# Norm factors spread from eight columns, the causal mask moved into VectorE's scan, and row 0 of each attention item scored half an item further ahead

## The reference, cut to what matters

```python
def rmsnorm(x, g):
    y = x * lax.rsqrt(jnp.mean(x * x, axis=-1, keepdims=True) + EPS)
    return y * g
# stick-breaking, for a block of queries at positions t
mask = key_pos[None, :] < t[:, None]
z = jnp.einsum("bhqd,bhkd->bhqk", qb, kf) * scale
log_keep = jnp.where(mask, jax.nn.log_sigmoid(-z), 0.0)
later = lax.cumsum(log_keep, axis=3, reverse=True) - log_keep
log_a = jax.nn.log_sigmoid(z) + later
a = jnp.where(mask, jnp.exp(log_a), 0.0)
out = jnp.einsum("bhqk,bhkd->bhqd", a, vf)
```

## Time and profile before

| | us |
|---|---|
| device time, median of 3 runs | 2651.57 (2646.75 to 2653.51) |
| span of the profiled execution, first to last instruction | 2646.9 |
| TensorE busy in that span | 2562.6 (97%) |
| VectorE, ScalarE, GpSimd busy | 1784.0, 1204.7, 719.9 |
| mean granted TensorE clock | 0.989 |

### The profile page before, as it was taken

The page is one execution under the profiler, slowest core; times in us unless marked ns, Lnnn a source line. Parts: engine busy times, 40 slices in busy tenths (PEclk is TensorE's granted clock), DMA queues, the critical chain, the costliest instruction groups (busy, mean ns, idle before and its releaser), DMA issues.

```text
span 2646.9 us, 34791 instructions
## 1 busy us (share of the span) xinstructions
PE 2562.6 (97%) x12320; PEld 2130.7 (80%) x12320; DVE 1784.0 (67%) x2247; ACT 1204.7 (46%) x2027; POOL 719.9 (27%) x523
## 2 busy tenths in 40 slices
PE   8899999999999999999999999998899999999999
PEld 8688887888888887887878888886788888887887
DVE  6566666167756577775677777777648665758667
ACT  6463333144434443335666666665424443444332
POOL 2502220102323222233033333333120322222322
PEclk9899999999999999999999999999999999999999
DMA  6412225213433456534111111112321342437634
GB/s 208 152 40 72 78 90 191 80 63 116 146 116 119 151 177 246 217 147 159 49 37 33 33 32 32 32 32 107 125 101 53 139 161 77 152 133 273 236 145 157
DMA packets 85923, 311.39 MB, mean 118 GB/s; under 512 B 10417, under 2 KB 10417, under 8 KB 73137
## 3 DMA queue, kind: packets, MB, share of 16 engines
q1 hardware_dynamic: 74304, 261.17, 28.0%
q0 software_dynamic: 11216, 42.47, 4.5%
q10 hardware_dynamic: 288, 6.29, 0.6%
HBM read 220.24 MB, written 89.65 MB: 117 GB/s over the span
## 4 chain that ended last, share of the span: by engine, by line
PE 79%; DVE 7%; issue 7%; ACT 4%; POOL 1%; DMA 1%; SPq 0%; ACTq 0%; DVEq 0%; POOLq 0%
PE ps L2334 25%; PE ps L2336 24%; PE ps L2335 24%; PE ps L2646 1%; POOL sig L968 1%; DVE aT_lo L1955 1%; PE ps L2662 1%; DVE tile_lo L2203 1%; DVE w_lo L1584 1%; DVE keep L1913 1%; ACT keep L1313 1%; PE ps L2663 1%; PE ps L2595 1%; ACT sq L1325 1%; PE ps L2596 1%
## 5 line engine op out<-in xcount | busy, mean ns | idle before, releaser
L2334 PE MATMUL ps<-tile_hi,g_hi 128*128 128x512 f32 x1680 | 661.3, 394 | 7.7 <-DVE tile_lo L2203 5.2
L2336 PE MATMUL ps<-tile_hi,g_lo 128*128 128x512 f32 x1680 | 658.3, 392 | 0.0
L2335 PE MATMUL ps<-tile_lo,g_hi 128*128 128x512 f32 x1680 | 654.7, 390 | 0.0
L2334 PE MATMUL ps<-xg_hi,w_hi 128*128 128x512 f32 x1024 | 412.6, 403 | 4.5 <-DVE xg_lo L1783 3.3
L2336 PE MATMUL ps<-xg_hi,w_lo 128*128 128x512 f32 x1024 | 402.6, 393 | 0.0
L2335 PE MATMUL ps<-xg_lo,w_hi 128*128 128x512 f32 x1024 | 402.1, 393 | 0.0
L2334 PEld LDWEIGHTS ps<-tile_hi,g_hi 128*128 128x128 f32 x1680 | 316.2, 188 | 76.1 <-issue 5.5
L2336 PEld LDWEIGHTS ps<-tile_hi,g_lo 128*128 128x128 f32 x1680 | 316.0, 188 | 71.5
L2335 PEld LDWEIGHTS ps<-tile_lo,g_hi 128*128 128x128 f32 x1680 | 316.3, 188 | 69.0
L1482 ACT ACTIVATE g_hi<-quads 128x512 fp32r<-128x512 f32 x310 | 194.9, 629 | 359.0 <-PE ps L2336 328.8
L2132 DVE TENSOR_TENSOR g_lo<-quads,g_hi 128x512 fp32r<-128x512 f32 x310 | 281.4, 908 | 107.1 <-ACT g_hi L1482 103.1
(11 more groups left out here) (277 smaller groups left out, 4338.4 us busy)
## 6 DMA issues: line engine op xcount, KB each, us to landing
quads<-wpack SPq DMA_DIRECT2D x62, 1024.0 KB, 5.9
raw<-wpack SPq DMA_DIRECT2D x88, 512.0 KB, 3.3
d_split<-x SPq DMA_DIRECT2D x116, 256.0 KB, 6.3
tile_lo<-d_tile SPq DMA_DIRECT2D x30, 512.0 KB, 7.5
d_tile<-R SPq DMA_DIRECT2D x46, 256.0 KB, 6.4
d_tile<-x SPq DMA_DIRECT2D x46, 256.0 KB, 6.1
cquads<-wpack SPq DMA_DIRECT2D x10, 1024.0 KB, 4.8
tile_hi<-d_split SPq DMA_DIRECT2D x10, 1024.0 KB, 8.5
```

The lines of the kernel that those rows point to most:

```text
L2334: pe.matmul(out, whi, mhi, start=start, stop=False, skip_group_check=chained)
L2335: pe.matmul(out, whi, mlo, start=False, stop=False, skip_group_check=chained)
L2336: return pe.matmul(out, wlo, mhi, start=False, stop=stop, skip_group_check=chained)
```

## The change

**Spread.** `diagonal`, `diag` and `kdiag` are gone. `spread_factors` now takes for each of the 8 blocks the column `recip[:, j]`, broadcast over 128 columns, as stationary operand, and the identity as moving one, so 8 float32 products of 128 columns take the place of 2 of 512. In the cross-attention it is moved behind `scores(1)` and goes to banks 2 and 3; `scores(0)` no longer waits for `R`, batch 1 does; `qstat(1)` and `query_root(1)` move to batches 1 and 2; ScalarE does `exps(0)` ahead of the copy to `R`. GpSimd's four differences are cut into 16 of 128x512 and start when the first `query_root` is done.

**Mask.** L2597 is gone. The scan's second operand is `fence`, zero but for an identity in the last 128 columns, and it computes state = state x keep + fence from 0 on: row p stays zero until column p of the last block, where it becomes 1. `sig` lies right-aligned with a last column that is zero for good, and ScalarE writes one column less.

**Order.** Item `it` now scores row 1 of item it + 1 at its start and row 0 of item it + 2 later on: behind the first fill (t = 0, 1), behind `turn` of the last chunk (t = 2, 3), at the very end in item 4 of the last pair. ScalarE and VectorE follow that order, ahead of the q and k copies and low parts. Row 0 of item 1 is done before the first pair. In the first pair two fills of `fence` (a memset and a copy) are added on VectorE and four one-column memsets on GpSimd.

```diff
+        def row_ahead(it, j):
+            return divmod(2 * (it + 1) + 1 + j, 2)
 # GpSimd, layer 0
-                    a11, a21, a12, a22 = c_sum[0], c_sum[1], c_sum[3], c_sum[6]
-                    part(0, a11, a11, a21, ALU.subtract)
...
+                    pool.wait_ge(rq_ready, 1)
+                    for k in range(4):
+                        a11, a21, a12, a22 = (c_sum[q][:, k, :] for q in (0, 1, 3, 6))
+                        part(4 * k, a11, a11, a21, ALU.subtract)
...
 # ScalarE, a pair
+                            ahead(0)
+                            for c in range(min(t + 1, 2)):
+                                chunk(hp, it, c, first)
+                            if t < 2 and not late:
+                                ahead(1)
...
+                            if t >= 2:
+                                ahead(1)
 # VectorE
-                        dve.tensor_tensor_scan(k, k, k, 1.0, ALU.mult, ALU.bypass).then_inc(scanned, 1)
+                        dve.tensor_tensor_scan(k, k, ones[:, width - n:width][:, ::-1], 0.0, ALU.mult, ALU.add
+                                               ).then_inc(scanned, 1)
-                diagonal(diag, diag_ready)
 # TensorE
-                for h in range(2):
-                    last = pe.matmul(ps[:, b + h, :], mean_head[:], src[:, 4 * h:4 * h + 4, :].rearrange("p a c -> p (a c)"),
-                                     start=True, stop=True)
+                for j in range(KB):
+                    last = pe.matmul(ps[:, b + j // 4, j % 4 * P:(j % 4 + 1) * P], recip[:, j:j + 1].to_broadcast([P, P]),
+                                     ident[:], start=True, stop=True)
-                pe.wait_ge(diag_ready, 2 * i + 1)
-                spread_factors(diag, 4, spread)
-                qstat(1)
                 scores(0)
+                pe.wait_ge(recip_ready, LAYERS + 2 * i + 1)
                 scores(1)
+                pe.wait_ge(rqv_ready, MHEADS * i + 1)
+                spread_factors(2, spread)
                 quarter_unit(2, 1)
                 for n in range(BATCHES):
-                    if n in (5, 9):
+                    if n == 1:
+                        pe.wait_ge(r_ready, 2 * i + 1)
+                    if n in (1, 5, 9):
                         qstat(1 + n // 4)
-                        pe.matmul(o[:, w - P:w], ident_r[:], mask_r[:], start=False, stop=True).then_inc(z_full, 1)
+                        scored.then_inc(z_full, 1)
+                                if not last and (item, r) in ((2, 1), (6, 0), (6, 1)):
+                                    pe.wait_ge(evacuated, hp * 6 + (v0 + 6 + (1 if item == 2 else 3 + r)))
...
+                            ahead(0)
                             for c in range(min(t + 1, 2)):
                                 turn(hp, it, c, par, first)
-                            for r in range(2):
-                                fill(counts[r])
+                            fill(counts[0])
+                            if t < 2 and not late:
+                                ahead(1)
+                            fill(counts[1])
...
+                                if t >= 2 and c + 2 == t:
+                                    ahead(1)
```

More of the change, by code:

```diff
@@ L245, in trunk @@
         cg_lo = [place(f"cg_lo{q}", [P, HALF], F32R, at + 2 * K1) for q, at in enumerate(ring)]
-        keep = place("keep", [P, 2, 2, SEQ], F32, 0)
-        sig = place("sig", [P, 2, 2, SEQ], F32, 16 * K1)
+        ROW = (SEQ - P, SEQ)
+        row_at = [[4 * sum(ROW) * par + 4 * ROW[0] * r for r in range(2)] for par in range(2)]
+        keep = [[place(f"keep{par}{r}", [P, ROW[r]], F32, row_at[par][r]) for r in range(2)] for par in range(2)]
+        sig = [[place(f"sig{par}{r}", [P, ROW[r]], F32, 15 * K1 + row_at[par][r]) for r in range(2)] for par in range(2)]
+        o_sum = place("o_sum", [P, 2, 2 * P], F32, 30 * K1)
         sq = place("sq", [P, 3, SEQ], F32R, Z)
@@ L259, in trunk @@
         aT_lo = place("aT_lo", [P, 2, 2, 2 * P], F32R, ME + 4 * K1)
-        o_sum = place("o_sum", [P, 2, 2 * P], F32, ME + 8 * K1)
-        o_low = place("o_low", [P, 2 * P], F32, ME + 10 * K1)
+        fence = place("fence", [P, SEQ], F32, ME + 12 * K1)
+        o_low = place("o_low", [P, 2 * P], F32, ME + 20 * K1)
         tf = place("tf", [P, SEQ], F32, ME + 16 * K1)
@@ L961, in _ @@
                         pool.dma_start(d_me[:, h, :], me_f[:, h, :]).then_inc(me_stored, 16)
+                    pool.wait_ge(x_spilled, 16)
+                    for par in range(2):
+                        for r in range(2):
+                            pool.memset(sig[par][r][:, ROW[r] - 1:ROW[r]], 0.0).then_inc(edges_made, 1)
                     def weigh(row, par, r, t):
@@ L976, in pair @@
                                     pool.dma_start(fp(mf_lo[:, h, :]), d_me[:, h, :]).then_inc(rows_back[h], 16)
-                            if not (last and it == ITEMS - 1):
-                                for r in range(2):
-                                    weigh(hp * ROWS + (2 * (it + 1) + r), (it + 1) % 2, r, (it + 1) % 4)
+                            for j in range(2):
+                                item, r = row_ahead(it, j)
+                                if not (last and item >= ITEMS):
+                                    weigh(hp * ROWS + (2 * item + r), item % 2, r, item % 4)
                             if not last:
@@ L1345, in pair, with ahead @@
                             t, hh = it % 4, it // 4
[L1346 to L1351, removed]
+                            def ahead(j):
+                                item, r = row_ahead(it, j)
+                                if not (last and item >= ITEMS):
+                                    sigmoids(hp * ROWS + (2 * item + r), item % 2, r, item % 4)
+                            late = last and it == ITEMS // 2
+                            ahead(0)
[3 more added lines that the diff above has]
+                                ahead(1)
                             if not last and it in (0, 3, 7):
@@ L1980, in pair, with ahead @@
                                     finished(r)
-                            if not (last and it == ITEMS - 1):
-                                for r in range(2):
-                                    row = hp * ROWS + (2 * (it + 1) + r)
-                                    scan(row, (it + 1) % 2, r, (it + 1) % 4)
-                                    if r == 0:
-                                        for c in range(min(t + 1, 2)):
-                                            chunk(hp, it, c)
-                                    finished(r)
+                            def ahead(j):
+                                item, r = row_ahead(it, j)
+                                if not (last and item >= ITEMS):
+                                    scan(hp * ROWS + (2 * item + r), item % 2, r, item % 4)
+                            late = last and it == ITEMS // 2
+                            if not (last and it == ITEMS - 1):
+                                ahead(0)
+                                for c in range(min(t + 1, 2)):
+                                    chunk(hp, it, c)
+                                finished(0)
+                                if t < 2 and not late:
+                                    ahead(1)
+                                finished(1)
                             if not last and it in (0, 3, 7):
@@ L2724, in pair @@
+                            late = last and it == ITEMS // 2
+                            counts = FILL_LAST[it] if last else FILL[it]
+                            ahead(0)
                             for c in range(min(t + 1, 2)):
                                 turn(hp, it, c, par, first)
-                            for r in range(2):
-                                fill(counts[r])
+                            fill(counts[0])
+                            if t < 2 and not late:
+                                ahead(1)
```

137 lines of the change are left out of this document (63 added, 74 removed).

## The result

The changed kernel takes 2659.32 us (median of 7 runs, 2656.06 to 2665.83), the kernel before 2651.57 (7 runs, 2646.75 to 2654.97). The ratio is 1.0034, 95% interval 1.0024 to 1.0044: slower, by about 8 us, where 16 us less were forecast. The profiled executions agree: spans of 2657.6 and 2646.9.

What follows compares the result with a forecast made beforehand. TensorE was taken as the bound everywhere, losing waits for chains through ScalarE, VectorE and GpSimd. Pairs -8.4, last pair -1.5, layer 0 -5.5, layer 1 +1.0, key factors -1.3: -15.7 on 2646.9, so median 2636; range 2614 to 2660.

Steps and rivals of the forecast that it cites:

- Waits that go: In the seven pairs, TensorE's waits for `aT_lo` and `sig` all go: 3.9 us a pair.
- The last pair: Last pair: early row 0 helps, waits for a `piece` in items 5 and 6 grow; net -1.5 us, between -5 and +2.
- the early items: Last pair, first turns: no fill covers items 0 and 1, so early row 0 makes item 3 end some 2.9 earlier.
- The masks: In the score rows of the pairs, a mask costs 0.11 us, 16 of them 1.8 a pair; bound below 1.0 a pair.
- the sum: Per pair, masks -1.8, old waits -3.9, `tf` waits +1.1, first-`weighted` waits +3.4: -1.2 us; seven pairs -8.4.
- The new waits: Items 2 and 6 of the pairs: evacuation waits add 1.1 us a pair, waits at the first `weighted` 3.4.
- S: Start of item 6 on TensorE, 1520.51 before; its chunk 0 of `aT_lo` was forecast ready at S + 6.0 to 6.7.
- Slower: Rival: first `weighted` of items 2 and 6 becomes the bound; no change at waits of 2.8, 2660 at 3.4; chance 0.13.
- The scan: VectorE's scan with an added second operand keeps its 2.31 us for 1024 elements; bounds 1.2 and 3.5.
- The spread: Cross-attention and key factors: layer 0 -5.5 us, layer 1 +1.0, key factors -1.3; other four spreads hidden, nothing.
- Layer 1: Cross-attention of layer 1: `scores(0)` idles 2.7 us for the load of `v_lo`, then half clock; +1.0, between -3 and +2.
- The key factors: Second spread: its 1.32 us wait for `kdiag` goes, -1.3.

Runs made afterwards that it cites:

- chunks first: The changed kernel with ScalarE and VectorE doing chunks 0 and 1 of items 2 and 6 before the sigmoids and scan of the 1024 row; 2641.29 us, ratio 0.9958.
- repaired kernel: The changed kernel with chunks 0 and 1 before the scan, q copies behind item 3's chunks and last-pair evacuations before scans; 2628.36 us, ratio 0.9910.
- q copies later: On top of chunks first, copies and low parts of q's second half moved from item 2's end behind item 3's chunks 0 and 1; 2634.84 us, ratio 0.9938.
- evacuations first: On top of chunks first, VectorE evacuates a finished piece before the scans in items 5 and 6 of the last pair; 2630.89 us, ratio 0.9920.
- masks kept: The repaired kernel with the mask products, the old scan and the old layout of `sig` put back; 2649.51 us, ratio 0.9991.

## Why the prediction was wrong

**Waits that go: the step that failed.** "I take all 3.9 a pair as gone." The waits for `sig` went, and so did those at the third `weighted`. The one in item 3 did not: from 0.33 it grew to 1.48, 1.6 with its drain, 11.5 us in seven pairs. I had walked the chain from the start of items 2 and 6, with their copies, and not that of item 3, where two copies of q stand in front as well and where TensorE lost the same score row. Shown: with those copies moved the wait falls from 1.18 to 0.43.

**The last pair: the second.** "Net -1.5, between -5 and +2"; it was +7.8. The wait for a piece in item 5 grew as forecast, and further (3.5 said, 4.34 measured). But the one in item 6 grew by 1.4 and not 0.6. The one of 0.78, which I had as held by the 1024 scan and going, stayed: in the trace of before VectorE had been idle for 1.77 in front of that evacuation, waiting for TensorE. And the early items saved nothing: where I had 2.9 less, the waits there went from 9.5 to 10.1, since the low parts of the memory (3.90) and the 1024 scan stand in a row in front of chunk 0 of item 2. All visible waits of the stretch grew by 4.7 (13.9 to 18.6). The other 3.0 are TensorE's own work, which took longer (66.84 to 69.86 busy) with the masks out, at a granted clock of 0.85 for 0.94. The waits of 5.03 and 4.34 are followed by products at the lower of the two levels, 1.2 GHz (granted 0.51 and 0.50 in the 4.5 us behind them; durations of 0.58 and 0.80 in the rows), and the one of 3.04 nearly so (0.58). I had priced the waits and not that. Shown for the scan (chunks first: 5.03 to 2.56) and for the evacuations (6.4 us of the last pair for 4.8 of waits); the low parts of the memory were not moved in any run. Three kernels with the old code in this stretch (before, the spread alone, the same with sixteen waits) took 80.9, 82.3 and 83.0, so some 2 us of it have no cause that I can name.

**The masks.** "So a mask costs 0.11, 16 of them 1.8 a pair, where nothing else holds TensorE". The condition was the error. A mask is 0.07 to 0.09 of busy time, 1.2 to 1.4 a pair, and more than half of it came back as waits for `aT_lo` and `sig`. By itself the edit gives 2 us (2645.55 to 2643.59, with intervals that overlap), in the repaired kernel nothing that the runs can tell, and by the profiles 0.5 a pair in both. With the sum's own way of counting, where the waits stand by themselves, 0.4 a pair of the miss are the masks'.

**The new waits.** Right: the first `weighted` of item 6 starts at S + 6.5 (1520.35 to 1526.89), said 6.0 to 6.7; its wait is 1.77, 1.9 with the drain, said 1.7; those for `tf` are 0.54 and 0.46, 0.7 and 0.6 with the drain, said 0.54. Together 0.7 a pair short. The rival "Slower" named this wait as the one that decides, from 2.8 up. It stayed at 1.9, so the time of that rival, 2660, came, but not by its mechanism: that the two agree is chance. By the sum, a pair: -1.2 said, +1.07 measured (66.80 to 67.87); the 2.3 are 1.6 of item 3, 0.7 of these and 0.4 of the masks, less 0.4 that this way of adding counts twice. Of the remaining 2 us of the seven pairs 1.5 lie in the second pair, where the granted clock was 0.81 from 1423.4 to 1432.6, and 0.4 are the score row at the bound.

**The scan.** Right: by its form no longer than before. The Trainium skill (DVE: opcode table, instruction layouts, handler registers and perf-mode slots, section Datapath and trigger behaviour) has the built-in scan at half throughput. The 2.29 us for 1024 elements agrees with that, as the 2.31 did.

**The spread.** Right: -5.3 in layer 0, and -6.1 as a whole (said -5.8), but the whole came out with two of its terms wrong in opposite ways. Layer 1 was +1.0 forecast and -0.7 measured: `v_lo` landed 8.9 after its issue, much as in the earlier trace rows, but TensorE came to `scores(0)` later than I had it, 9.8 from `norm` on where the same products took 8.0 before. The granted clock of the `norm` and `qstat` stretch was 0.76 and had been 1.00. So the idle time was 0.70, and low clock lay where I had counted a wait. The key factors' 1.32 went as a wait, but the stage ends no earlier (+0.1): the granted clock from 80 to 92 was 0.90 and had been 1.00. Why it was lower is open.

**The order, then,** was the loss: it costs 16 us with the masks out and 20 with them in. Most of that is a matter of what stands in front of the chunks on the helper engines: with chunks first, q copies later and evacuations first the same order gives a pair of 64.8, against 66.3 for the old order. No run makes these moves in the old order, so how much of the 1.5 is owed to the new order itself is not shown.

## What to carry to other kernels

When TensorE's order is moved, walk each item's first consumer and not only those whose waits you set out to remove: a stretch that gives away its cover gets every chain in front of it as a wait. A product that fills time while another engine is late is worth less than its length when it is taken out (here 0.5 us a pair for 1.2 to 1.4), so price it by the waits around it. On the helper engines, put what TensorE wants next ahead of what it wants an item later; three such moves turned a loss of 8 us into a gain of 23.

## What the runs showed of the hardware

TensorE can stand still at the start of a round of its loop for nothing that its waits name: 5.5 and 4.6 us in one kernel (spread alone), 7.7 and 7.4 in another (masks kept), in the second and third of three rounds, each followed by a stretch at a low clock (0.66 from 1530 to 1545 with the standstill in the first, 0.85 from 1537.8 to 1550 behind it in the second), so that a round took 9 to 10 us more. Sixteen satisfied waits in front of the loop, which compute nothing, took 14.4 us (2659.93 to 2645.55) and 20.6 us (2649.51 to 2628.86) off these kernels.

The profiles name what the waits column does not. The page lists a DMA queue that carries instructions (packets, MB, share). These are the rows of the masks-kept kernel and of the changed one:

```profile
q8 instruction: 82, 1.34, 0.2%
...
q8 instruction: 64, 1.05, 0.2%
```

The two kernels that stand still have 82 such packets, all twelve others 64, also the same two with the sixteen waits. In the kernel before none lands between 1530 and 1810: the second and third round run from what the first one brought. In the masks-kept kernel 18 land there, four of them between 1530 and 1541, around its first standstill. So three things are shown: only the kernels that stand still bring instructions again in the later rounds, packets of them fall around the standstills, and sixteen more instructions in front of the loop end both. That TensorE waits for these packets is the plain reading; the profile does not say whose queue this is. Why these two kernels bring their instructions again and the others do not stays open, beyond that it changes with where the instructions lie.

Whoever times an edit of a looped kernel should look for "issue" in TensorE's waits and at the packets of that queue before believing the number: without that look the spread's 6 us would have passed for a loss of 9.
